# First modulation on TensorE, and another order of work in the gathered experts of a transformer kernel

## What is computed

```python
cond = jax.nn.silu(c)
m = (cond @ w_mod[l] + b_mod[l]).reshape(bsz, 3, 3, D_MODEL)       # section 0 uses m[:, 0]
h = rmsnorm(x, g) * (1 + m[:, i, 1]) + m[:, i, 0]
...
def expert_block(args):                                            # one of 64 routed experts
    toks, e, wts = args
    out = swiglu_2(xpad[toks], w1[e], w3[e], w2[e])                # 1024 -> 256 -> 1024
    return out * wts[:, None]
```

## Time and profile before

| | |
|---|---|
| median of three runs | 3787.46 us (3784.85 to 3802.31) |
| the profiled execution | 3798.87 us, span 3796.9 us |
| TensorE busy (matmuls) | 3530.8 us, 93% of the span |
| VectorE busy | 2332.1 us, 61% |
| ScalarE busy | 1477.7 us, 39% |
| GpSimd busy | 240.3 us, 6% |
| DMA | 842.63 MB, mean 222 GB/s |
| mean granted TensorE clock | 0.964 |
| first product of section 0 | 94.89 us from the start |

### The profile page before, as it was taken

How to read it: one execution, slowest core, us unless ns; L and a number is a source line. 1 busy time by engine, 2 the same in 40 slices (tenths; PEclk the granted TensorE clock), 3 DMA queues, 4 the chain that set the end, 5 groups by cost and what they waited for, 6 DMA issues and landing times.

```text
span 3796.9 us, 52579 instructions
## 1 busy us (share of the span) xinstructions
PE 3530.8 (93%) x21065; PEld 2989.7 (79%) x21065; DVE 2332.1 (61%) x3517; ACT 1477.7 (39%) x2212; POOL 240.3 (6%) x337
## 2 busy tenths in 40 slices
PE   4999899999899998889999999999988999999999
PEld 2997799997699787789767676778778976766776
DVE  6774475775377474546666666656554766666666
ACT  1432233432143204133555555541232355555554
POOL 3010010010001000000000000000000000000000
PEclk9999899999899899889999999999998999999999
DMA  7785286784178552345889998875432688898986
GB/s 260 250 297 165 81 293 196 244 293 152 57 245 303 187 188 100 122 153 183 271 283 292 293 286 283 279 239 171 134 121 90 214 273 270 284 289 274 296 274 191
DMA packets 580320, 842.63 MB, mean 222 GB/s; under 512 B 22715, under 2 KB 489760, under 8 KB 578832
## 3 DMA queue, kind: packets, MB, share of 16 engines
q1 hardware_dynamic: 514508, 665.85, 53.5%
q0 software_dynamic: 41056, 147.35, 11.8%
q10 hardware_dynamic: 24548, 26.57, 2.8%
HBM read 836.37 MB, written 3.33 MB: 221 GB/s over the span
## 4 chain that ended last, share of the span: by engine, by line
PE 77%; DVE 9%; DMA 7%; ACT 3%; issue 2%; SPq 1%; DVEq 0%; ACTq 0%
PE bank L990 14%; PE bank L895 11%; PE bank L896 11%; PE bank L897 11%; PE bank L1336 8%; DMA ring<-in_w 3%; DMA far_up<-in_w 3%; PE bank L1349 2%; PE bank L1306 2%; PE bank L1307 2%; PE bank L1203 2%; PE bank L890 2%; PE bank L1301 2%; PE bank L1303 1%; PE bank L1302 1%
## 5 line engine op out<-in xcount | busy, mean ns | idle before, releaser
L897 PE MATMUL bank<-hh,ring_lo 128*128 128x256 f32 (+1 forms) x2176 | 621.7, 286 | 0.0
L895 PE MATMUL bank<-hh,hi 128*128 128x256 f32 (+1 forms) x1984 | 570.8, 288 | 16.7 <-issue 12.3
L896 PE MATMUL bank<-h_lo,hi 128*128 128x256 f32 (+1 forms) x1984 | 567.0, 286 | 0.0
L990 PE MATMUL bank<-h,ring 128*128 128x256 f32 x2432 | 556.4, 389 | 8.4 <-ACT h L1513 8.4
L990 PEld LDWEIGHTS bank<-h,ring 128*128 128x128 f32 x2432 | 475.7, 196 | 80.2 <-issue 12.1
L897 PEld LDWEIGHTS bank<-hh,ring_lo 128*128 128x128 f32 (+1 forms) x2176 | 419.9, 193 | 0.0
L895 PEld LDWEIGHTS bank<-hh,hi 128*128 128x128 f32 (+1 forms) x1984 | 382.7, 193 | 25.3 <-issue 17.6
L896 PEld LDWEIGHTS bank<-h_lo,hi 128*128 128x128 f32 (+1 forms) x1984 | 382.9, 193 | 0.5 <-issue 0.5
L895 PE MATMUL bank<-hid,hi 128*128 128x256 f32 (+1 forms) x1216 | 346.8, 285 | 2.2 <-DVE ring_lo L2592 2.2
L896 PE MATMUL bank<-hid_lo,hi 128*128 128x256 f32 (+1 forms) x1216 | 343.9, 283 | 0.0
L897 PE MATMUL bank<-hid,ring_lo 128*128 128x256 f32 (+1 forms) x1088 | 307.6, 283 | 0.0
(11 more groups left out here) (372 smaller groups left out, 6642.6 us busy)
## 6 DMA issues: line engine op xcount, KB each, us to landing
ring<-in_w SPq DMA_DIRECT2D x258, 1024.0 KB, 12.3
ring<-in_ffn_w SPq DMA_DIRECT2D x120, 1024.0 KB, 10.5
wmod<-in_w_mod POOLq DMA_DIRECT2D x216, 512.0 KB, 5.6
far_up<-in_w SPq DMA_DIRECT2D x84, 1024.0 KB, 13.1
ring<-in_w_in SPq DMA_DIRECT2D x74, 1024.0 KB, 6.0
work<-in_w SPq DMA_DIRECT2D x42, 1024.0 KB
ring<-in_w_out SPq DMA_DIRECT2D x16, 1024.0 KB, 5.1
ring<-in_w_mod SPq DMA_DIRECT2D x12, 1024.0 KB, 12.7
```

Source lines behind the costliest of these rows:

```text
L895: pe.matmul(o, w_hi, x_hi, start=start, stop=False, skip_group_check=True)
L896: pe.matmul(o, w_hi, x_lo, start=False, stop=False, skip_group_check=True)
L897: return pe.matmul(o, w_lo, x_hi, start=False, stop=stop, skip_group_check=True)
L990: ins = pe.matmul(o[:, half * T:(half + 1) * T], l_, r_, start=(k == 0), stop=(k == KD - 1))
```

## The change

Two independent parts.

**Setup.** GpSimd's and VectorE's sums of the first modulation go, and with them `sum_mods(0)`. TensorE makes the modulation itself: for each of the eight rows k, 16 products (a 128x128 block of the slab as stationary operand, one column of `cond` as moving) for shift and scale (`shift_and_scale`), and 8 more for the gate (`gate`), all accumulating in bank 3. They stand between the filter layers, after the squares' sum and after the vectors' turn, in TensorE's program order, with the norm's sum of section 0. The spectrum products get four banks of their own (4 to 7) and a wait for the input's copies (`x_done`); VectorE copies the spectrum out after the norm (`keep_spectrum`). SyncE loads the eight modulation slabs first and the four gate slabs behind them, each released by TensorE's progress. The small loads are issued by GpSimd, into `macc`. GpSimd clears `kz` after the last spectrum product and fetches `wmod` only then.

**Gathered units.** TensorE does `turn_few(n)` ahead of `finish(n-1)`; `hidden_few` gets a second buffer. ScalarE does `middle(n)` and `columns_hi(n+1)` first, then all four copies of `split_ups(n+1)`, then `turned_few(n)` and `out_hi(n-1)`. VectorE does `product` and `columns_lo(n+1)` first, then all four subtractions, then `spread_slots`, `hidden_few` and `out_lo(n-1)`. Dense units keep their order.

```diff
@@ setup, TensorE
+                def shift_and_scale(k):
+                    here(mod_slabs[k])
+                    for j in range(2 * KD):
+                        ins = pe.matmul(bank[3][:, j:j + 1], ring[:, mod_slabs[k][0], j * P:(j + 1) * P], cond[:, k:k + 1],
+                                        start=(k == 0 and j == 0), stop=(k == KD - 1), skip_group_check=True)
+                    ins.then_inc(first_mod, 1)
+
+                def gate(k):
+                    here(gate_slabs[k // 2])
+                    w = down_slab(gate_slabs[k // 2][0])[:, k % 2, :]
+                    for j in range(KD):
+                        ins = pe.matmul(bank[3][:, 2 * KD + j:2 * KD + j + 1], w[:, j * P:(j + 1) * P], cond[:, k:k + 1],
+                                        start=False, stop=(k == KD - 1), skip_group_check=True)
+                    ins.then_inc(mod_summed if k == KD - 1 else first_mod, 1)
+
+                pe.wait_ge(cond_done, 1)
+                shift_and_scale(0)
+                pe.wait_ge(filter_in, 16 * FILTER_LOADS)
+                filter_layer(0)
+                pe.matmul(bank[0][0:NQ, :], bkt[:, 0:NQ], bkt[:, 8:520], start=True, stop=True).then_inc(table_done, 1)
+                shift_and_scale(1)
                 turn_input()
+                filter_layer(1)
+                shift_and_scale(2)
+                filter_layer(2)
+                shift_and_scale(3)
+                shift_and_scale(4)
                 pe.wait_ge(f_sin, 3)
                 pe.wait_ge(spectrum_in, 16 * SPECTRUM_LOADS)
+                pe.wait_ge(x_done, KD)
...
+                for k in range(5, KD):
+                    shift_and_scale(k)
+                norm(0)
                 turn_vectors()
+                for k in range(KD):
+                    gate(k)
                 pe.wait_ge(f_norm, 4)
@@ gpsimd
+            pool.wait_ge(f_mm, 12)
+            pool.memset(kz[:, :, :], 0.0).then_inc(zeroed, 1)
             pool.wait_ge(zeroed, 5)
@@ routed, TensorE
                 def turn_few(n):
                     p, wide = GATHER_NO[n], ORDER[n][0] == "wide"
+                    pe.wait_ge(hid_done, t0 + 2 * n)
...
                         if gathers(n - 1) and gathers(n - 2):
                             scatter(n - 2)
+                        turn_few(n)
                         finish(n - 1)
-                        turn_few(n)
@@ routed, ScalarE
                     if gathers(n):
-                        split_ups(n + 1, 0)
                         middle(n)
                         columns_hi(n + 1)
+                        split_ups(n + 1, 0)
                         split_ups(n + 1, 1)
+                        turned_few(n)
                         out_hi(n - 1)
-                        turned_few(n)
@@ routed, VectorE
                         p = GATHER_NO[n]
-                        lo_ups(n + 1, 0)
                         if slots(n) == WIDE:
...
                         columns_lo(n + 1)
+                        lo_ups(n + 1, 0)
                         lo_ups(n + 1, 1)
-                        out_lo(n - 1)
                         spread_slots(n)
...
+                        out_lo(n - 1)
```

More of the change, by code:

```diff
@@ L443, in build @@
         ringplan = Ring()
-        gate_slabs = [ringplan.take((first_gate, k + 2)) for k in range(0, KD, 2)]
+        ringplan.align(3)
         mod_slabs = [ringplan.take((first_mod, k + 1)) for k in range(KD)]
+        gate_slabs = [ringplan.take((first_mod, KD + k + 2)) for k in range(0, KD - 2, 2)] + [ringplan.take((mod_summed, 1))]
         plan = []
@@ L696, in _ @@
                 load(q, down_slab(q[0]), mod_rows[:, k:k + 2, 2 * D:3 * D])
-            for k in range(KD):
-                if k == RING - 4:
-                    small_loads()
-                load(mod_slabs[k], ring[:, mod_slabs[k][0], :], mod_rows[:, k, 0:2 * D])
             for sec in plan:
@@ L763, in _ @@
         def _(pool):
-            pool.wait_ge(cond_done, 2)
-            for k in range(KD):
-                slot, count, _ = gate_slabs[k // 2]
-                pool.wait_ge(full[slot], count)
-                w, acc, c = down_slab(slot)[:, k % 2, :], macc[:, 2 * D:3 * D], cond[:, k:k + 1]
-                if k == 0:
-                    pool.tensor_scalar(acc, w, c, 1.0, ALU.mult, ALU.mult).then_inc(first_gate, 1)
-                else:
-                    pool.tensor_scalar(wmod[:, k % 2, :], w, c, 1.0, ALU.mult, ALU.mult).then_inc(gate_scaled, 1)
-                    pool.wait_ge(gate_scaled, k)
-                    pool.wait_ge(first_gate, k)
-                    pool.tensor_tensor(acc, acc, wmod[:, k % 2, :], ALU.add).then_inc(first_gate, 1)
@@ L841, in setup, with filter_layer @@
             def setup():
-                pe.wait_ge(filter_in, 16 * FILTER_LOADS)
-                for n, (w, rows) in enumerate(((fw1, 33), (fw2, 64), (fw3, 64))):
+                def filter_layer(n):
+                    w, rows = ((fw1, 33), (fw2, 64), (fw3, 64))[n]
                     if n:
@@ L2648, in routed @@
                             dve.wait_ge(product_done, g0 + p + 1)
-                            dve.tensor_tensor(hidden_few[:, 0:P], product[:, 0:P], bank[1][:, P:2 * P], ALU.mult).then_inc(hid_done, 2)
+                            dve.tensor_tensor(hidden_few[p % 2][:, 0:P], product[:, 0:P], bank[1][:, P:2 * P], ALU.mult).then_inc(hid_done, 2)
+                        out_lo(n - 1)
                     else:
@@ L2672, in _ @@
                 norm(sec)
+                if s == 0:
+                    keep_spectrum()
                 if s == 6:
```

137 lines of the change are left out of this document (56 added, 81 removed).

## The result

| | before | after |
|---|---|---|
| median | 3787.84 us (3784.85 to 3802.31) | 3902.27 us (3900.29 to 3905.68) |
| profiled execution | 3798.87 us | 3904.07 us, span 3902.1 us |
| mean granted TensorE clock | 0.964 | 0.957 |
| first product of section 0 | 94.9 us | 139.2 us |
| turnarounds, summed in layer one and in layer two | 256.7 and 266.4 us | 286.0 and 286.0 us |

The changed kernel takes 1.0303 times as long, with a 95% interval of 1.0283 to 1.0324: 114 us more, where the forecast had 79. The forecast lies in the right direction and the time is inside its range, but one of its terms was a fourth of what it should have been.

The account below looks back on a forecast made before the run. TensorE's program order, busy 93% of the span, was taken to bound the kernel. Gathered turnarounds +50, lowered clock +20 and setup +9 gave +79 us: 3866 us against the median, range 3808 to 3920.

Parts of the forecast that it names:

- turnarounds: From the end of a gathered unit's up products to the start of the next gathered unit's; together +50 us.
- The chain of four subtractions: Gathered units: columns, then four subtractions behind the up products set the turnaround, at 6.92, 7.02 or 7.54 us.
- The first rival: Gathered units: the subtractions don't bind and TensorE's own work is the turnaround; -55, 3732 us; 10%.
- the second (weights stay late): Gathered units: the next loads start later, so the relief of 33.5 us is missing; +112, 3900 us; 8%.
- the relief: Narrow units ahead of wide ones: late weights no longer delay fourteen turnarounds, giving back 33.5 us in both layers.
- The clock behind the new pauses: Gathered units behind dense ones: pauses of about 2.6 us lower TensorE's clock; +20 us, bounds 0 and 31.
- The third rival: Gathered units: the clock falls in every turnaround, not only behind the 18 long pauses; +179, 3966 us; 8%.
- Dense units, outputs, `turn_few`'s wait: Gathered stages: turnarounds into dense units, the outputs moved last and the wait for `hid_done` cost nothing.
- The setup: Before section 0: products at 0.22 us, section 0 starts at 105.6 instead of 94.89; net +9 us.
- The landing of `axial`: Setup: the load that `turn_input` waits for lands at 39 us, bounds 34 and 43, instead of 35.0.
- My upper bound of +20: Setup: the most its +9 us term was allowed to cost; the lower bound was -5.
- The small loads and `wmod`: Setup loads on GpSimd: small loads cost 0, at most +10; `wmod` lands before it is wanted, 0, at most +4.

Follow-up runs that it names:

- the second trace of before: The kernel before run once more with no edit, for a second trace: 3779.82 us, one run, beside 3778.17.

## Why the prediction was right, and where not

**The chain of four subtractions.** Right, to the hundredth: 6.92, 7.02 and 7.54 us were forecast, 6.91, 7.01 and 7.53 measured, in all classes, and the run with one subtraction early moved them by 1.13. By class and layer: behind dense units +20.4 (forecast +20.5), wide behind gathered +13.5 and +13.6 (+13.6), narrow ahead of narrow +6.3 and +6.6 (+6.5), narrow ahead of wide -11.0 and -20.9 (-10.8 and -20.7). The first rival (the subtractions don't bind) fell by this, the second (weights stay late) by the same rows: no turnaround is over 7.53. But the relief is partly a trait of the execution that was read: set against the second trace of before it is 23.5 us and not 31.8 (84.2 and 89.9 less 150.6).

**The clock behind the new pauses.** Right in size. Forecast: 16 stretches at 1.3 us, +20. In the changed kernel 13 of the 18 turnarounds behind a dense unit are followed by up products at the lower level, and none of the 62 others; before, none of the 18. Ten of the 13 are 1.55 us longer (5.52 us for 3.97, 7.38 for 5.84), two 1.3 and 1.4, and one 2.8. Behind the pauses of 2.44 to 2.60 us the level was lower in 11 of 12 cases, behind those of 2.17 us in 2 of 6. The one with 2.8 us, stretches of after just ahead of and in the up products at 2272.64:

```profile
2265.00:2272.00 7.00, 4.71 (x38) 3.99 (x36) 5.29 (x7) 5.10 (x8) 0.95 (x1) 1.00 0.43 107
2272.60:2279.40 6.80, 6.76 (x17) 5.07 (x17) 0.16 (x1) 0.00 (x0) 0.00 (x0) 0.54 1.06 372
```

The third rival (a fall in every turnaround) fell: in the 62 others, with pauses of 1.53 us and less, the clock stayed.

**Dense units, outputs, `turn_few`'s wait.** Costed at nothing; all that the gathered stages lost beside turnarounds and up products is 2.3 us in both layers. The turnarounds into a dense unit sum to 94.1 us before and after.

**The setup.** Here the step that failed is the price of a product. I took 0.22 us from one stretch at full clock and wrote that from the landing on TensorE is never free for long. I took for granted that being busy keeps the clock up, though the 24 one-column products of the earlier trace rows had taken 6.26 us, 0.26 each and not 0.22. The trace of before had the reason: the level fell in their midst, with TensorE busy throughout. Two stretches of before, the products from 84.26 on:

```profile
84.30:88.60 4.30, 4.30 (x41) 4.30 (x40) 3.46 (x4) 2.31 (x3) 0.00 (x0) 1.00 0.92 228
88.80:90.50 1.70, 1.70 (x9) 1.64 (x8) 0.57 (x1) 1.42 (x2) 0.00 (x0) 0.50 1.14 358
```

In the changed kernel the clock is at its lower level for 27.3, 13.7 and 23.9 us of the 96.5, with no pause in them, and the neighbours pay too: the spectrum's first products 7.19 us for 3.70, the squares' sum 5.73. Term by term against the forecast: shift and scale 2 to 4 18.1 us for 10.5, spectrum and squares 12.9 for 7.2, shift and scale 5 to 7 15.6 for 10.5, norm 5.5 for 3.7, gates 23.2 for 14.1, the last spectrum products 16.1 for 13.9: 31.5 us more by rows that overlap a little, 29.9 by the stretch. The run with 128 columns throughout shows the cause, since it changes nothing in the setup but the columns and brings the forecast's terms back (10.88, 3.70, 14.48 and 13.90 us). The landing of `axial` adds 3.7 (42.70 for 39, inside the bounds), and the run that waits for the identity alone shows that it counts in full. Some 3.0 of the 7.7 us by which it is later than before are a later issue, at 15.33 us on ScalarE's queue for 12.32. My upper bound of +20 had no room for the clock at all, and that the time lies in the stated range is owed to the width of the other terms. Only the third rival had a dear clock, and that in the gathered units.

The Trainium skill (TensorE: Matmul & The Clock Gate, section HAM oscillation) puts a lowered clock down to waits between bursts of products. For the gathered units the traces agree: 13 stretches, each behind a pause of 2.17 to 2.60 us. In the setup they don't: the clock fell in stretches where TensorE's records leave no gap.

**The small loads and `wmod`.** Right: the turn of the vectors at 99.42 didn't wait, and section 1 takes 160.4 us (160.5 before). The small loads are under way together with `axial`, though, which may be why its landing took 27.3 us for 22.7; that wasn't tried.

**The sum.** +79 forecast, +105 in the profiled executions: +34 from the setup, +2 clock, +2 rest of the stages, -1 turnarounds, -1 other sections, and -10 from sections 6 and 8, which the second trace of before has as well. Against the medians it is +114, because the profiled execution of before stood 11 us above its median, that of after 2.

## What to carry to other kernels

Work that moves to TensorE is to be priced with the clock that it leaves behind, for itself and for what stands next to it: here products of one column cost 0.227 us at the upper level, the same as with 128 columns, but the level fell to 0.50 in their course and the neighbours paid as well. When an order answers the critical engine first, count what then stands behind that answer: here four subtractions of 1.14 us behind some 2.2 us of columns, against 4.4 to 7.4 us of TensorE's own work (the turnarounds of after less the pauses in them). Take a reordering apart before judging it: of this one, TensorE's half gains 20 us and ScalarE's and VectorE's half on top of it loses 87 (3859.34 against 3772.44), and with one part early and three behind the loss is gone (3769.06 beside 3782.86, one run). Count the stages and not only the turnarounds: of 35.6 us won there, the two stages kept 2.9. And read a second execution of the kernel before where the sum rests on late transfers.

## What the runs showed of the hardware

- TensorE busy without a gap in its records sat at the lower clock: 27 us at 0.50 in the changed kernel, 61.4 us where one-column and 512-column products alternate.
- A float32 product of 128x128 took the same time at one level of the clock with few and many moving columns: 0.43 us at the lower with one (13.81 us for 32) and with 16 (13.83), 0.227 and 0.226 at the upper with one and with 128. In these setups the level fell with one column and with 16, and with 128 it stayed.
- Pauses of 2.17 to 2.60 us ahead of the up products were followed by the lower level in 13 of 18 cases, and in 9 of 18 in the run with the gathered units alone; those of 1.53 us and less, 62 in each of the two, never were.
